# First modulation third by column halves, and a first projection in two sums, in a two-layer diffusion trunk

## The reference, cut to what matters

```
mod   = silu(c) @ w_ada[l] + b_ada[l]            # w_ada[l]: 1024 x 6144
sh1, sc1, g1, sh2, sc2, g2 = split(mod, 6)
h     = x * (1 + sc1) + sh1                      # the same for the context, with c_ctx
qkv, gates = split(h @ w_in[l])                  # then three attention branches
x     = layer_norm(ALPHA * x + g1 * mix(...))
x     = layer_norm(ALPHA * x + g2 * moe(x * (1 + sc2) + sh2))
```

## Time and profile before

| | us |
|---|---|
| median of 3 runs | 1797.87 |
| lowest and highest run | 1793.67, 1799.39 |
| span of the profiled execution | 1798.2 |

### The profile page before, as it was taken

The page is one execution under the profiler, slowest core; times in us unless marked ns, Lnnn a source line. Parts: engine busy times, 40 slices in busy tenths (PEclk is TensorE's granted clock), DMA queues, the critical chain, the costliest instruction groups (busy, mean ns, idle before and its releaser), DMA issues.

```text
span 1798.2 us, 22841 instructions
## 1 busy us (share of the span) xinstructions
PE 1538.2 (86%) x9600; PEld 805.9 (45%) x9600; DVE 499.2 (28%) x1073; ACT 389.1 (22%) x859; POOL 26.1 (1%) x49
## 2 busy tenths in 40 slices
PE   6999999999997998899888698999967667776764
PEld 2544446888654343433222364468643333332322
DVE  0224776333342000011010544865330000100003
ACT  1213676221222010200000132764210001000000
POOL 1000000000000000000000100000000000000000
PEclk8999999999998999999999899999977777877676
DMA  9545821333529999999999811035969999999995
GB/s 386 206 176 234 313 65 60 110 99 123 224 94 395 422 422 421 421 421 421 421 422 422 318 44 47 1 123 188 357 267 422 420 421 421 421 420 421 421 421 223
DMA packets 98180, 522.80 MB, mean 291 GB/s; under 512 B 10768, under 2 KB 13088, under 8 KB 42784
## 3 DMA queue, kind: packets, MB, share of 16 engines
q1 hardware_dynamic: 94384, 509.97, 70.6%
q0 software_dynamic: 3392, 10.85, 1.8%
q10 hardware_dynamic: 304, 0.53, 0.1%
HBM read 520.17 MB, written 1.15 MB: 290 GB/s over the span
## 4 chain that ended last, share of the span: by engine, by line
PE 56%; SPq 19%; DMA 15%; DVE 7%; ACT 1%; issue 1%; DVEq 0%; ACTq 0%
PE psum L513 52%; SPq L1001 19%; DMA ring<-in_w_down 6%; DMA ring<-in_w_up 4%; PE psum L563 4%; DMA A<-in_w_down 2%; DMA A<-in_w_up 2%; DMA ring<-in_w_ada 1%; DVE small L1598 1%; DVE X L1713 1%; DVE PR L1618 1%; DVE X L1630 1%; DVE X L1629 0%; ACT hT L1146 0%; DVE stats L1719 0%
## 5 line engine op out<-in xcount | busy, mean ns | idle before, releaser
L513 PE MATMUL psum<-ring,A 128*32 128x256 f32 (+2 forms) x2112 | 364.1, 555 | 71.5 <-DMA ring<-in_w_up 36.8
L513 PEld LDWEIGHTS psum<-ring,A 128*32 128x32 f32 (+2 forms) x2112 | 124.8, 142 | 288.9 <-issue 146.0
L513 PE MATMUL psum<-A 128*32 128x256 f32 (+5 forms) x1152 | 212.5, 520 | 38.4 <-DMA A<-in_w_up 20.7
L513 PE MATMUL psum<-ring_r,h_hi 128*128 128x512 f32 x576 | 179.9, 394 | 5.8 <-DVE h_lo L1786 5.8
L513 PE MATMUL psum<-ring,PR 128*32 128x256 f32 (+1 forms) x1080 | 149.7, 522 | 31.6 <-DMA ring<-in_w_down 31.5
L513 PE MATMUL psum<-ring,hT 128*128 128x512 f32 (+3 forms) x512 | 164.9, 477 | 7.5 <-ACT hT L1146 7.3
L1749 DVE TENSOR_TENSOR W<-W,psum 128x512 f32<-128x512 f32 (+1 forms) x32 | 17.7, 554 | 545.7 <-PE psum L513 545.7
L513 PEld LDWEIGHTS psum<-A 128*32 128x32 f32 (+3 forms) x1152 | 70.6, 142 | 125.9 <-issue 55.4
L513 PEld LDWEIGHTS psum<-ring_r,h_hi 128*128 128x128 f32 x576 | 109.5, 190 | 29.6 <-issue 6.6
L513 PEld LDWEIGHTS psum<-ring,hT 128*128 128x128 f32 x512 | 87.0, 195 | 73.4 <-issue 69.3
L513 PE MATMUL psum<-ring_r,h_lo 128*128 128x512 f32 x288 | 113.2, 393 | 0.0
(11 more groups left out here) (191 smaller groups left out, 1406.3 us busy)
## 6 DMA issues: line engine op xcount, KB each, us to landing
ring<-in_w_down SPq DMA_DIRECT2D x93, 1024.0 KB, 26.0
ring<-in_w_up SPq DMA_DIRECT2D x84, 1024.0 KB, 25.3
ring<-in_w_gate SPq DMA_DIRECT2D x81, 1024.0 KB, 25.3
ring<-in_w_ada SPq DMA_DIRECT2D x48, 1024.0 KB, 11.8
A<-in_w_up SPq DMA_DIRECT2D x41, 1024.0 KB, 26.0
A<-in_w_gate SPq DMA_DIRECT2D x37, 1024.0 KB, 26.7
ring<-in_w_in SPq DMA_DIRECT2D x36, 1024.0 KB, 5.1
A<-in_w_down SPq DMA_DIRECT2D x28, 1024.0 KB, 26.0
```

The costliest lines, as they stand in the source:

```text
L513: return nc.tensor.matmul(o, a, b, start=start, stop=stop, skip_group_check=True)
```

## The change

The first third of layer 0 is loaded in two column halves q = 0, 1: each has 512 columns of sh1 and the same 512 of sc1, so half 0 is all that the feature slices k = 0 to 3 of every tile need. A piece is now 256 rows (two k) by 2 x 512 columns, in two DMAs with 2 KB per row. A piece is 16 matmul instructions of 256 columns instead of 8 of 512. The copy, the turn and the columns are done once for each half.

Then chunk 1 of w_in is multiplied in two sums. With half 0 in, all four tiles are transposed for slices 0 to 3, ScalarE modulates them, and `first_half` adds slices 0 to 3 of each tile into a bank of its own (four banks, left open), with the four pieces of half 1 multiplied after each. After the turn of half 1, VectorE modulates slices 4 to 7, and the P(1, t) steps add the other four slices. x's transfer is issued when half 0 is in. The bias is transposed first. The steps are in the order of `QKV_STEPS`. In the diff below, the last two stretches are ScalarE's and VectorE's programs, the one with `second_half` is the P step in `qkv`.

```
-            for k in range(KT):
-                if k == 4:
-                    pe.wait_ge(context_in, 16)
-                    for _, t in H_EARLY:
-                        x_transposes("hT", 0, t)
-                ada_products(0, 0, k)
...
-            ada_turn(0, 0)
+            for kk in range(4):
+                first_products(0, kk)
+            first_turn(0)
+            pe.wait_ge(context_in, 16)
+            for t in (0, 1):
+                x_transposes("hT", 0, t, (0, ))
+            for t in (2, 3):
+                pe.wait_ge(x_in, 16)
+                x_transposes("hT", 0, t, (0, ))
+            for t in (0, 1):
+                x_transposes("hT", 0, t, (1, ))
+            a, w = CHUNKS[1][0]
+            n, first_in = piece([w_in[0, 0:512, a:a + w]], 4, w)
+            for t in range(4):
+                ins = first_half(t, first_in)
+                if t == 3:
+                    free(n, ins)
+                first_products(1, t)
+            first_turn(1)
+            for t in (2, 3):
+                x_transposes("hT", 0, t, (1, ))
...
+            def first_products(q, kk):
+                if kk == 0:
+                    begin(("ada", 0, "first", q), bank=ADA_BANK)
+                cols = slice(FIRST_WIDTH * q, FIRST_WIDTH * q + FIRST_WIDTH)
+                src = w_ada[0, 256 * kk:256 * kk + 256, 0:2 * D].rearrange("(j p) (c n) -> p j c n", j=2, c=2)
+                n, w = piece(tuple(((slice(0, P), slice(0, 2), c), src[:, :, c, cols]) for c in (0, 1)), 2, 2,
+                             FIRST_WIDTH)
+                for j in (0, 1):
+                    k = 2 * kk + j
+                    for g in range(4):
+                        ins = mm(psum[32 * g:32 * g + 32, ADA_BANK, 0:256], cs[:, k, :],
+                                 w[:, j, g // 2, 256 * (g % 2):256 * (g % 2) + 256], k == 0, k == KT - 1)
...
+            def first_turn(q):
+                drained(pe, ("ada", 0, "first", q))
+                b = begin(("adaT", 0, "first", q), bank=TURN_BANK)
+                for j in (0, 1):
+                    ins = nc.tensor.transpose(psum[:, b, P * j:P * j + P],
+                                              modrow[:, 256 * q + P * j:256 * q + P * j + P], ident)
+                end(ins, b)
...
+            def first_half(t, w):
+                b = begin(("P", 0, 1, t), takers=2)
+                drained(pe, ("hT", 0, t, 0))
+                for k in range(KT // 2):
+                    ins = mm(psum[:, b, :], hT[:, k, t * P:(t + 1) * P], w[:, k, :], k == 0, False)
+                return ins
...
+                        second_half = l == 0 and ch == 1
+                        if second_half:
+                            b = groups["P", l, ch, t][0]
+                        else:
+                            b = begin(("P", l, ch, t), takers=2 if ch != 0 else 1)
...
+                        k_first = KT // 2 if second_half else 0
+                        for k in range(k_first, KT):
...
-            pool.wait_ge(slot_filled[7], 16)
+            pool.wait_ge(slot_filled[3], 32)
             pool.dma_start(X[:, 2:4, :], x.rearrange("b (t p) d -> p (b t) d", p=P)).then_inc(x_in, 16)
...
                 if l == 0:
-                    pool.wait_ge(slot_filled[1], 32)
+                    pool.wait_ge(slot_filled[0], 48)
...
-            ada_move(0, 0)
+            first_move(0)
+            act.wait_ge(mod_cols, 1)
+            for t in range(4):
+                modulated("hT", 0, t, SC1, SH1)
+            first_move(1)
...
-            ada_columns(0, 0)
+            first_columns(0)
+            first_columns(1)
+            for t in range(4):
+                modulated("hT", 0, t, SC1, SH1)
```

More of the change, by code:

```diff
@@ L421, in load @@
                     pieces[n] = part({"A": A, "B": B}[home], at, *shape)
-                loads[s] += 1
+                loads[s] += len(src) if isinstance(src, tuple) else 1
                 counts[n] = 16 * loads[s]
@@ L526, in ada_products @@
                     free(n, ins)
+            def first_products(q, kk):
[10 more added lines that the diff above has]
+                                 w[:, j, g // 2, 256 * (g % 2):256 * (g % 2) + 256], k == 0, k == KT - 1)
+                if kk == 3:
+                    free(n, event=end(ins, ADA_BANK))
+                else:
[13 more added lines that the diff above has]
+                return ins
             def ada_turn(l, third):
@@ L564, in transposes, with x_transposes @@
                 end(ins, b)
-            def x_transposes(name, l, t):
-                for j in (0, 1):
+            def x_transposes(name, l, t, halves=(0, 1)):
+                for j in halves:
                     transposes((name, l, t, j), [X[:, t, k * P:(k + 1) * P] for k in range(4 * j, 4 * j + 4)])
@@ L575, in qkv @@
                     if kind == "H":
[L576 to L580, removed]
+                        pe.wait_ge(x_ready, 2 * first_tile(l - 1) + len(tiles(l - 1)) + t + 1)
                         x_transposes("hT", l, t)
@@ L586, in qkv @@
                             held = []
-                        b = begin(("P", l, ch, t), takers=2 if ch != 0 else 1)
+                        second_half = l == 0 and ch == 1
+                        if second_half:
+                            b = groups["P", l, ch, t][0]
+                        else:
+                            b = begin(("P", l, ch, t), takers=2 if ch != 0 else 1)
                         lo = 384 if cut and ch in (0, 2) else 0
@@ L597, in qkv @@
                                                   width))
-                            w, o = held[k // 4][1][:, k % 4, lo:], psum[:, b, lo:width]
+                            w, o = held[(k - k_first) // 4][1][:, k % 4, lo:], psum[:, b, lo:width]
                             if cut and ch == 1:
@@ L977, in _ @@
             end(nc.tensor.transpose(psum[:, b, 0:48 * DEPTH], bias_rows[:, :], ident[0:48 * DEPTH, 0:48 * DEPTH]), b)
-            ada_turn(0, 0)
+            for kk in range(4):
[14 more added lines that the diff above has]
+                if t == 3:
+                    free(n, ins)
+                first_products(1, t)
+            first_turn(1)
+            for t in (2, 3):
+                x_transposes("hT", 0, t, (1, ))
             step = QKV_TURNS
             for l in range(DEPTH):
-                qkv(l, PE_FIRST + QKV_NEXT if l else FIRST_STEPS)
+                qkv(l, PE_FIRST + QKV_NEXT if l else QKV_STEPS)
                 for s in streams(l):
@@ L999, in _ @@
                 landed = slot_filled[slot_of[n]]
-                if not isinstance(src, list):
+                if not isinstance(src, (list, tuple)):
                     sp.dma_start(dst, src).then_inc(landed, 16)
+                    continue
+                if isinstance(src, tuple):
+                    for where, rows in src:
+                        sp.dma_start(dst[where], rows).then_inc(landed, 16)
                     continue
@@ L1116, in _, with first_move @@
                 .then_inc(bank_drained[b], 1)
+            def first_move(q):
+                b = filled(act, ("ada", 0, "first", q))
+                nc.scalar.copy(modrow[:, 256 * q:256 * q + 256], psum[:, b, 0:256]).then_inc(bank_drained[b], 1)
             def ada_move(l, third):
                 b = filled(act, ("ada", l, third))
-                if (l, third) != (0, 0):
-                    filled(act, ("adaT", *divmod(3 * l + third - 1, 3)))
+                before = divmod(3 * l + third - 1, 3)
+                filled(act, ("adaT", *before) if before != (0, 0) else ("adaT", 0, "first", 1))
                 nc.scalar.copy(modrow[:, :], psum[:, b, :]).then_inc(bank_drained[b], 1)
@@ L1161, in qkv @@
                         if t == 0:
-                            act.wait_ge(mod_cols, 1 if l == 0 else 6)
-                        modulated("hT", l, t, SC1, SH1, (0, 1) if l and t < 2 else (0,))
+                            act.wait_ge(mod_cols, 7)
+                        modulated("hT", l, t, SC1, SH1, (0, 1) if t < 2 else (0,))
                     if kind == "P":
@@ L1298, in _ @@
                 n_gates = 6 * first_tile(l)
-                qkv(l, ACT_FIRST + QKV_NEXT if l else H_EARLY + FIRST_STEPS)
+                qkv(l, ACT_FIRST + QKV_NEXT if l else QKV_STEPS)
                 if l == 0:
@@ L1402, in mark, with first_columns @@
                 V_.engine_nop().then_inc(sem, 1)
+            def first_columns(q):
+                b = filled(dve, ("adaT", 0, "first", q))
+                src = psum[:, b, 0:256].rearrange("p (j c g r) -> p c g j r", j=2, c=2, g=2)
+                bias = bias_cols[:, 0:16].rearrange("p (c q g j) -> p c q g j", c=2, q=2, g=2)[:, :, q, :, :]
+                for s in (0, 1):
+                    dst = modcol[:, 0, s, 0:16].rearrange("p (c q g j) -> p c q g j", c=2, q=2, g=2)[:, :, q, :, :]
+                    ins = V_.tensor_tensor(dst, src[:, :, :, :, s], bias, ALU.add)
+                run(ins)
+                mark(bank_drained[b])
```

(3 more changed lines are left out.)

10 lines of the change are left out of this document (4 added, 6 removed).

## The result

| | before | changed |
|---|---|---|
| median of 18 runs, us | 1797.96 | 1803.14 |
| lowest and highest | 1792.96, 1801.16 | 1797.55, 1807.16 |
| span of the profiled execution | 1798.2 | 1797.7 |

The ratio is 1.0027 with a 95% interval of 1.0019 to 1.0035. The change costs 5.2 us by the medians (the interval is 3.4 to 6.3). It is clearly slower, and just inside the 0.3% that I called no difference. The forecast was 1803.8.

A forecast was written before the change was run, and what follows sets the result against it. The edited stage was taken as a DMA wait, then TensorE setting the pace. x landing at 28.9, 35.6 of listed work, 3.8 pieces and 5.1 turn gave +4.6 us; bank 1.3 made +5.9: 1803.8 us, range 1797 to 1810.

The forecast's parts named there:

- The loads: First-half pieces of w_ada: 2 KB rows at 386 GB/s, four pieces in at 18.0 us.
- x's first packet: GpSimd's queue: from issue of x's transfer to its first packet 4.1 us, read from the trace.
- x's transfer: x's 1.05 MB beside w_in and w_ada on the other queue: 200 GB/s, 5.2 us.
- The rival with one packet each: Queues alternate packets, x takes 3.9 us: +4.6 us, 1802.5; chance 0.25 shared with the clock staying high.
- The low clock after the wait for x: TensorE starts after 5 us of idleness, so 2.1 us of low clock is charged, as before the change.
- The narrow pieces: Four second-half pieces standing between the half products on TensorE: 4 x 0.95 = 3.8 us added.
- The split products: Chunk 1 products split into two sums: same 16 instructions together, so no added time.
- The gap: Turn between the halves, with copy, transposes and VectorE's modulation, all exposed on TensorE: 5.1 us added.
- A clock that falls in it: Rival: clock falls in the turn between halves, first second half runs low: 2.1 us more, +8.0, 1805.9; chance 0.11.
- The bank: P(3,0) must wait for VectorE to read bank 3, just filled by P(1,3): 1.3 us more.
- The shift stays: A shift at P(3,0) counts in full at the end, since later weights are issued late too.
- The rival on the other side: Not slower: x doesn't set the products' start; 2.6 us less than the old kernel, 1795.3; chance 0.10.

The follow-up runs named there:

- x_2k: Changed kernel with x loaded in two transfers of 512 columns each, rows of 2 KB, TensorE waiting for both; ratio 1.0030 to the kernel before, median 1803.68 us.
- x_early: Changed kernel with x's transfer issued when the second piece of the first column half is in, not the fourth; ratio 1.0006 to the kernel before, median 1799.63 us.
- second profile: The changed kernel run and profiled once more without any edit; ratio 1.0030 to the kernel before, median 1803.23 us.
- reorder: Changed kernel with half products 0 and 1 before the wait for x, turn before half product 3, banks set by hand; ratio 0.9963 to old kernel, 1791.95 us.
- three: Changed kernel with x issued at the second piece, turn before half product 3, and a bank skipped before P(3,0); ratio 0.9964 to old kernel, 1791.14 us.
- gap: Changed kernel with second-half pieces moved between earlier half products and the turn placed before half product 3; ratio 1.0002 to the kernel before, median 1798.34 us.
- late: Changed kernel with the half products moved behind the second half's turn, so none runs during its loads; ratio 1.0012 to the kernel before, median 1800.37 us.
- bank: Changed kernel with one bank of the turn left out so P(3,0) takes bank 4, not 3; ratio 1.0016 to the kernel before, median 1800.79 us.

## Why the prediction was right

The time (1803.14 against 1803.8), the sign and the mechanism were right; that the time came out so near is in part luck, as the terms show. The chances were worse placed: I gave slower by over 0.3% 0.52 and within 0.3% 0.43, and the 5.2 us are 0.29%. By its steps:

- **The loads.** The fourth piece was in for the product at 17.54 (18.0 said), x's issue at 17.80, at 386 GB/s for the 2 KB rows as taken from w_in.
- **x's first packet**: said 4.1 us after the issue. In the changed kernel the queue had its first 3 packets in 21.5 to 22 us, 3.7 to 4.2 us after it. The figure of the Trainium skill ("DMA: Bandwidth & Descriptors", Latency and other measured facts) of about 1 us for the first byte of a GpSimd-issued transfer is off by 3 us here, where the DMA engines were busy throughout (105.0% at 18 to 20 us); by it the forecast would have been about 1801.
- **x's transfer**: said 5.2 us at half the bandwidth, measured 3.9 (about 22.0 to 25.9), the lower bound. This is the one term that was sized from the wrong row: at 1019 to 1020 the other queue had 102 packets against 56, and I took that for the rule. Why the counts were uneven there isn't shown; GpSimd's queue was then fed by eight transfers of 3 to 384 KB. The row that applied was that of 8 to 12 us with its even counts, as the context's transfer shows (run x_2k). The rival with one packet each was right. The rule of the Trainium skill (the same page, Queues, rings and completion order) of a packet from each queue in turn agrees with the even counts, if the trace's packets are the page's, and not with those of 1019 to 1020.
- **Last packet to landing**: 1.6 said, 0.8 measured (25.9 to 26.66). x was in at 26.7, not 28.9, 2.2 us earlier.
- **The low clock after the wait for x**: 2.1 us said. In the first profile the 16 transposes took 3.24 where 2.2 is the full clock's, thus 1.0; in the second 3.47 and 1.27 in the half product, thus 2.5. But the wait isn't shown to be its cause, as the prediction had it. The eight transposes before the wait took 1.92 us, where eight take 1.04 to 1.09 at the full clock, so the clock was low already. And x_early, without the wait, lost 1.6 us in its 24 transposes (4.69 against 3.07).
- **The narrow pieces**: 3.8 us said; a piece and its hand-over take 1.00 (47.36 to 48.36), 4.0 in all.
- **The split products**: put at nothing ("their two halves have the same 16 instructions together"). From each one's start to TensorE's next instruction, the eight half products take 28.6 us in the first profile. The old kernel's whole ones take 6.96 each at the full clock, 27.8 for four. That is 0.8 us for the split.
- **The gap**: 5.1 said, 4.7 measured (48.36 to 53.08). A clock that falls in it I had made a rival with 0.11. It happens in three of five profiles, at a price of 0.7 to 1.7 us in the half product and, in two of the three, 0.4 us in the transposes. That rival should have had half of the chance, and a smaller price than 2.1 us.
- **The bank**: 1.3 said, 1.22 to 1.23 measured, and the run with a free bank removes it.
- **The shift stays**: 3.7 us at P(3, 0), 3.9 at 293.5; in the second profile 6.4 and, from the chain there, 6.6. Behind that, single profiles differ by several us either way and can't show it. The medians do: from reorder and three (P(3, 0) at 63.49 and 64.62, 1791.95 and 1791.14 us) over gap, x_early and late (69.98 to 71.53, 1798.34 to 1800.37) to the changed kernel (73.82 and 76.51, 1803.14), the time follows the mark, with bank (74.77, 1800.79) the one off the line.

So the sum of +5.9 us is near the measured 5.2, but its terms err both ways. At P(3, 0) the first profile has 3.7: x is 2.2 us earlier than said, the low clock 1.1 less and the gap 0.4 less, and against that stand the split products with 0.8 and the pieces with 0.2. The second profile has 6.4: the clock took back 2.7 there. The median lies between the two, and that it lies so near the forecast is luck.

The rival on the other side, that x doesn't set the start, fell with x_early. The price that I had worked out for an x that costs nothing, 2.6 us below the old kernel, was too good: x_early ended at 1.0006, with P(3, 0) at 71.16, 1.0 us after the old kernel's. Its half products began about 1.0 us later than in that sum, which had no low clock, the clock in the gap cost 1.7 us and the split 0.8. From that price I had also concluded that a gain over 0.3% was out of reach of the mechanism. This was wrong. With the gap and the bank's wait removed as well it is 0.36% (three), and 0.37% with x's transfer as late as ever (reorder). What I had missed is that the gap, the bank and the wait for x belong to the order of the program and not to the split.

## What to carry to other kernels

Cutting a load in two to start earlier only pays if what the program does first has all that it needs: one transfer left behind on another queue (x here) sets the start instead. Either ask for it earlier, or put the work that doesn't need it ahead of the wait; both gave the same here. The cut also makes a second hand-over between engines; put it ahead of the last piece of independent work, not behind it, or it stands open on the critical engine and may cost its clock besides. Count the banks that are held open across the cut: the next taker in turn can be the one just filled.

## What the hardware showed that I had not expected

- Packet for packet, the queue with the bigger packets gets the more bytes. The context came in with a third of the bytes beside 8 KB rows and with two thirds beside 2 KB rows, so narrower rows on one queue sped up a transfer on the other.
- In x_2k, x's packets held 3.7 KB on the average though its rows are 2 KB, as if GpSimd's queue put two rows into a packet; SyncE's 2 KB rows were packets of 2 KB (0.77 MB in 393).
- In the second profile of the changed kernel the granted clock stands at 1.00 from 26 to 34 us, but the half product at 30.14 took 4.87 us instead of 3.60. In the first 30 us or so of these profiles the durations show the lower level where the column of the granted clock doesn't, so there the durations must be read.
- The same stretch of 10 small instructions in 4.7 us lost the clock in three executions and kept it in two. What decides it isn't shown.
